# Ring slots by age, a router per token, and the first expert's rows gathered by quarters in a two-layer hybrid backbone

## The reference

```python
def _moe(h, router_w, w_gate, w_up, w_down):
    logits = (h @ router_w).astype(jnp.float32)
    top_v, top_i = lax.top_k(logits, TOP_K)
    top_w = jax.nn.softmax(top_v, axis=-1)
    gates = jnp.einsum('btk,btke->bte', top_w, jax.nn.one_hot(top_i, N_EXPERTS, dtype=jnp.float32)).astype(h.dtype)
    out = jnp.zeros_like(h)
    for e in range(N_EXPERTS):
        out = out + gates[..., e:e + 1] * _swiglu(h, w_gate[e], w_up[e], w_down[e])
    return out
...
        x = x + g1 * _rms_norm(y, norm_g[1])
        h2 = _modulate(_rms_norm(x, norm_g[2]), sh2, sc2)
        x = x + g2 * _rms_norm(ffn(h2), norm_g[3])
```

## Time and profile before

| what | us |
|---|---|
| median of 3 runs (1684.74 to 1691.21) | 1684.79 |
| profiled execution, its own time | 1685.35 |
| its span, first to last instruction | 1683.8 |
| TensorE busy | 1618.1 |
| VectorE busy | 1065.2 |
| ScalarE busy | 930.3 |
| mean granted clock of TensorE, share of full speed | 0.992 |

### The profile page before, as it was taken

One profiled execution on the slowest core, in us unless ns is written; L12 is line 12 of the kernel. 1 busy time (PEld: TensorE's weight loads), 2 busy tenths in 40 slices (PEclk: granted clock), 3 DMA queues, 4 the chain that ended last, 5 costly groups with the idle time before them and its releaser, 6 DMA issues.

```text
span 1683.8 us, 22722 instructions
## 1 busy us (share of the span) xinstructions
PE 1618.1 (96%) x8388; PEld 1296.7 (77%) x8388; DVE 1065.2 (63%) x1372; ACT 930.3 (55%) x1328; POOL 37.9 (2%) x60
## 2 busy tenths in 40 slices
PE   4999999899999999899997999999999999999997
PEld 2884469698888888688685888888888888888885
DVE  5442432532222333553655989999999999999998
ACT  4413332632222322552564777787778778787775
POOL 0000000040000000000001000000000000000000
PEclk9999999999999999999999999999999999999999
DMA  8623672696222222352134999999999999999982
GB/s 325 222 75 125 250 275 76 250 350 242 87 97 100 100 100 100 140 203 99 51 128 180 419 391 397 380 369 392 361 399 360 399 352 405 375 368 394 371 340 77
DMA packets 67850, 426.24 MB, mean 253 GB/s; under 512 B 8640, under 2 KB 12480, under 8 KB 19776
## 3 DMA queue, kind: packets, MB, share of 16 engines
q1 hardware_dynamic: 60000, 396.93, 61.2%
q0 software_dynamic: 7776, 28.32, 4.3%
HBM read 401.62 MB, written 23.59 MB: 253 GB/s over the span
## 4 chain that ended last, share of the span: by engine, by line
PE 91%; DVE 4%; ACT 2%; DMA 1%; issue 1%; SPq 0%; ACTq 0%; DVEq 0%
PE ps L1713 27%; PE ps L1715 26%; PE ps L1714 26%; PE ps L1731 2%; PE ps L1756 2%; PE ps L1888 1%; DMA raw<-in_w 1%; PE ps L2199 1%; PE ps L1949 1%; DVE small L1262 1%; PE ps L1932 1%; PE ps L1921 1%; DVE raw L1428 0%; DVE wl L1020 0%; PE ps L1953 0%
## 5 line engine op out<-in xcount | busy, mean ns | idle before, releaser
L1560 DVE TENSOR_TENSOR wl<-raw,wh 128x1024 fp32r<-128x1024 f32 x522 | 615.6, 1222 | 63.6 <-ACT wh L924 56.9
L924 ACT ACTIVATE wh<-raw 128x1024 fp32r<-128x1024 f32 x522 | 524.9, 1057 | 97.6 <-PE ps L1715 97.6
L1713 PE MATMUL ps<-wh,ah 128*128 128x512 f32 (+1 forms) x800 | 311.0, 389 | 2.3 <-issue 1.8
L1713 PE MATMUL ps<-ah,wh 128*128 128x512 f32 (+1 forms) x848 | 302.1, 356 | 9.5 <-DVE al L1137 6.0
L1715 PE MATMUL ps<-wh,al 128*128 128x512 f32 (+1 forms) x800 | 302.4, 378 | 0.0
L1714 PE MATMUL ps<-wl,ah 128*128 128x512 f32 (+1 forms) x800 | 301.6, 377 | 0.0
L1714 PE MATMUL ps<-al,wh 128*128 128x512 f32 (+1 forms) x848 | 293.8, 346 | 0.0
L1715 PE MATMUL ps<-ah,wl 128*128 128x512 f32 (+1 forms) x848 | 293.8, 346 | 0.0
L1020 DVE TENSOR_TENSOR wl<-raw,wh 128x1024 fp32r<-128x1024 f32 x120 | 141.6, 1221 | 116.9 <-ACT wh L500 116.9
L1713 PEld LDWEIGHTS ps<-ah,wh 128*128 128x128 f32 x848 | 161.4, 190 | 37.1 <-issue 6.9
L1714 PEld LDWEIGHTS ps<-al,wh 128*128 128x128 f32 x848 | 161.5, 190 | 20.4 <-issue 0.7
(11 more groups left out here) (260 smaller groups left out, 1489.1 us busy)
## 6 DMA issues: line engine op xcount, KB each, us to landing
raw<-in_w SPq DMA_DIRECT2D x372, 1024.0 KB, 6.2
sent<-raw POOLq DMA_DIRECT2D x16, 512.0 KB, 24.5
back<-raw POOLq DMA_DIRECT2D x16, 512.0 KB, 25.3
x<-sent POOLq DMA_DIRECT2D x7, 512.0 KB, 12.2
back<-x POOLq DMA_DIRECT2D x7, 512.0 KB, 8.6
x<-in_x SPq DMA_DIRECT2D x2, 1024.0 KB, 9.0
raw<-in_ukv SPq DMA_DIRECT2D x1, 1024.0 KB, 7.2
out<-raw SPq DMA_DIRECT2D x4, 256.0 KB, 3.3
```

The source lines that it names most:

```text
L924: act.activation(wh[:, J % SPLITS, piece_half(h)], slot(J % SLOTS)[:, piece_half(h)], ACT.Copy).then_inc(w_hi, 1)
L1560: ins = dve.tensor_tensor(wl[:, J % SPLITS, piece_half(h)], slot(J % SLOTS)[:, piece_half(h)], wh[:, J % SPLITS, piece_half(h)].bitcast(F3 ...
L1713: pe.matmul(out, lh, rh, start=start, stop=False)
```

## The change

**Slots.** `ring_slots` gives each ring entry the slot whose last entry is oldest, out of an allowed set. Fillers 14 to 30 and a few beside them may also use slots 7 and 8, once the projections have read them (`proj_ps`); fillers 31 to 39 and main 13 to 15 also slot 9, once the attention is over (`mla_pv`). The entries around layer one's feed-forward now wait for these:

| entry | slot before, waits for | slot after, waits for |
|---|---|---|
| main 13 | 1, main 12 split | 0, filler 28 used |
| main 14 | 1, main 13 split | 2, filler 32 used |
| filler 35 | 2, filler 33 used | 0, main 13 split |
| filler 36 | 0, filler 34 used | 1, filler 33 used |
| filler 37 | 1, main 14 split | 9, filler 34 used |
| filler 38 | 2, filler 35 used | 2, main 14 split |
| filler 39 | 0, filler 36 used | 0, filler 35 used |

SyncE issues in the order of the list, so an entry also waits for those ahead of it. ScalarE's split of main 14 moves ahead of the last two squares.

**Router.** The norm N_O2 with its sums on TensorE is gone. TensorE turns the unscaled `x` and multiplies it, per token, with a router that was multiplied by a beforehand. ScalarE squares the turned tokens with an accumulated sum per token, makes the root on two numbers per partition, and scales the turned tokens by it (`plain_tok`, no a, no b). The residual goes by pairs of chunks. `keep_busy` puts matmuls whose result nobody reads on TensorE at two places. The diagonal matrix, L2116 and `shiftB` are gone.

**Gather.** Expert 0's rows are gathered from `plain_tok` in four quarters in four banks; ScalarE applies a and b there (features are on partitions again) and rounds, VectorE takes the low part, and the first two pieces of `gate_up` wait for each quarter.

**Sent tokens.** They need a and b along the free axis. GpSimd writes a and b to memory (`flat_rows`) and reads them back to all partitions; VectorE multiplies and adds them after the selection, in between the quarters. Row numbers come after, the gates behind the first hidden product. The turn of the last expert's selection and the loads of the token count move to the end.

```diff
+        elif RING_AT["mod", ATT_MODS] <= p < RING_AT["main", M_GU + 3]:
+            allowed = OUT_SLOTS
+        last = {j: max([q for q in range(p) if slots[q] == j], default=-1) for j in allowed}
+        slots.append(min(allowed, key=last.get))
...
             out_unit(6)
+            split(M_GU + 1)
             for k in range(6, KD):
                 stream_square(N_E2L, k)
             root(N_E2L)
-            split(M_GU + 1)
...
+            for n, (a, b) in enumerate(ss_parts):
+                act.wait_ge(sem("tok_ps"), n + 1)
+                for t in range(2):
+                    act.activation(plain_part(t, a, b), by_pairs(turned(t, a, b)), ACT.Square, accum_out=tok_ss[:, t, n:n + 1]).then_inc(sem("tok_squared"), 1)
+            act.wait_ge(sem("tok_summed"), 1)
+            act.activation(tok_rinv, tok_sum, ACT.Ln, bias=eps[:, 0:1], scale=1.0 / D).then_inc(sem("tok_ln"), 1)
...
+                for k in range(KD):
+                    q, cols = k // 2, slice((k % 2) * P, (k % 2 + 1) * P)
+                    act.wait_ge(sem("first_ps"), q + 1)
+                    act.activation(xe_first[q][:, cols], ps[:, first_banks[q], cols], ACT.Identity,
+                                   bias=mod1[:, 24 + k, 0:1], scale=scl[:, 1, 2, k, 0:1]).then_inc(sem("xe_v"), 1)
...
+                counted(N_OY, p, dve.tensor_tensor(pair(tmp[p % 2]), y_o[:, two, :], rinv[:, None, 0:TL].broadcast_to([P, 2, TL]), ALU.mult))
+                dve.wait_ge(t_ready, T_AT[N_OY, p] + 1)
+                dve.tensor_tensor(x[:, two, 0:TL], x[:, two, 0:TL], pair(tmp[p % 2]), ALU.add).then_inc(res_done, 1)
...
+            def scaled_token(t):
+
+                dve.wait_ge(sem("rows_spread"), 16 * 2)
+                dve.wait_ge(sem("tok_f32"), 3 + t)
+                dve.tensor_tensor(tok_rows(t), plain_tok[t], scale_rows, ALU.mult).then_inc(sem("tok_scaled"), 1)
...
-                    first_gathered()
+                    scaled_token(0)
+                    scaled_token(1)
+                    first_gathered(0)
+                    shifted_token(0)
+                    first_gathered(1)
+                    shifted_token(1)
+                    first_gathered(2)
+                    row_numbers()
+                    first_gathered(3)
                     first_split(2)
                 split_next(0, AHEAD)
                 hidden(0, at.hid + 1)
                 if not no:
-                    dve.wait_ge(sem("back_sel_ps"), 1)
-                    dve.tensor_copy(back_sel_T, ps[:, 2, 0:TL]).then_inc(sem("back_sel_T"), 1)
+                    gates()
...
+            pool.wait_ge(sem("last_scales"), 1)
+            pool.wait_ge(w_used, M_OIN + OIN)
+            for n, columns in enumerate((scl[:, 1, 2, :, 0], mod1[:, 24:24 + KD, 0])):
+                pool.dma_start(flat_rows[n].rearrange("(k p) -> p k", p=P), columns, allow_slow_non_contiguous=True).then_inc(sem("rows_flat"), 16)
+            pool.wait_ge(sem("rows_flat"), 16 * 2)
+            for n, dst in enumerate((scale_rows, shift_rows)):
+                pool.dma_start(dst, flat_rows[n:n + 1, :].rearrange("o (a n) -> o a n", a=4).broadcast_to([P, 4, TL])).then_inc(sem("rows_spread"), 16)
...
             pe.wait_ge(evac_act, evacs(("t", 3), "act"))
+            keep_busy(6, 2)
             for k in range(KD):
-                sum_square(N_O2, k)
-                pe.wait_ge(sem("x_scaled"), k + 1)
-                mm = pe.matmul(ps[0:NE, 5, 0:TL], router[:, k, :], scaled_x[:, k, :], start=(k == 0), stop=(k == KD - 1))
...
+                for t in range(2):
+                    mm = pe.matmul(ps[:, 5, t * NE:(t + 1) * NE], x[:, k, t * P:(t + 1) * P], router[:, k, :], start=(k == 0 and t == 0), stop=(k == KD - 1 and t == 1))
+            mm.then_inc(sem("logits_ps"), 1)
+            keep_busy(6, 4)
```

More of the change, by code:

```diff
@@ L37 @@
 HEADS = 4
+N_PROJ = 2 * HEADS + HEADS // 2 + 4
 QR, KVR = 3, 2
@@ L99, with ring_slots @@
 FIRST_SLOTS = (7, 8, 3, 9, 0, 1, 2, 3, 9, 2)
-RING_SLOT = [FIRST_SLOTS[p] if p < len(FIRST_SLOTS) else (p - len(FIRST_SLOTS) + 1) % EARLY_SLOTS for p in range(len(RING))]
+ATT_SLOTS, OUT_SLOTS = (0, 1, 2, 7, 8), (0, 1, 2, 9)
+def ring_slots():
+    slots = list(FIRST_SLOTS)
+    for p, e in enumerate(RING):
+        if p < len(FIRST_SLOTS):
+            continue
+        allowed = tuple(range(EARLY_SLOTS))
+        if RING_AT["mod", NORM_MODS + 2] <= p < RING_AT["main", M_WOUT + 3]:
+            allowed = ATT_SLOTS
+        elif RING_AT["mod", ATT_MODS] <= p < RING_AT["main", M_GU + 3]:
+            allowed = OUT_SLOTS
+        last = {j: max([q for q in range(p) if slots[q] == j], default=-1) for j in allowed}
+        slots.append(min(allowed, key=last.get))
+    return slots
+RING_SLOT = ring_slots()
 VEC = {}
@@ L329, in build @@
         y_o = area(0, KD, TL)
-        scaled_x = x[:, :, TL:T]
+        plain_tok = [x[:, 4 * t:4 * t + 4, TL:T] for t in range(2)]
         xeh, xel = (a[:, 4:6, :].rearrange("p a b -> p (a b)").rearrange("p (k s) -> p k s", k=KD) for a in (ah, al))
@@ L354, in build, with by_pairs, plain_part, turned @@
         half_ss = small[:, 16:20]
+        tok_ss, tok_sum = small[:, 64:70].rearrange("p (t n) -> p t n", t=2), small[:, 72:74]
+        ss_parts = ((0, 4), (4, 6), (6, KD))
+        def by_pairs(v):
+            return v.rearrange("p (a n) -> p a n", n=TL)
+        def plain_part(t, a, b):
+            return plain_tok[t][:, a // 2:b // 2, :]
+        def turned(t, a, b):
+            bank, first = (2 * t, 0) if a < 4 else (2 * t + 1, 4) if a < 6 else (7 - 3 * t, 6)
+            return ps[:, bank, (a - first) * P:(b - first) * P]
         vecs_loaded = sem("vecs_loaded")
@@ L888, in _ @@
             root(N_OY)
-            for k in range(KD):
-                squares(N_O2, lambda k: x[:, k, 0:TL], lambda k: act.wait_ge(res_done, 4 * KD + k + 1), chunks=(k,))
-                act.activation(scaled_x[:, k, :], x[:, k, 0:TL], ACT.Copy, scale=scl[:, 1, 2, k, 0:1]).then_inc(sem("x_scaled"), 1)
-            root(N_O2)
+            for n, (a, b) in enumerate(ss_parts):
[4 more added lines that the diff above has]
+            act.activation(tok_rinv, tok_sum, ACT.Ln, bias=eps[:, 0:1], scale=1.0 / D).then_inc(sem("tok_ln"), 1)
+            act.wait_ge(sem("tok_ln"), 1)
+            act.activation(tok_rinv, tok_rinv, ACT.Exp, scale=-0.5).then_inc(sem("tok_root"), 1)
+            act.wait_ge(sem("tok_root"), 1)
+            for t, h in tok_parts:
+                for a, b in ss_parts[h:2 * h + 1]:
+                    ins = act.activation(plain_part(t, a, b), by_pairs(turned(t, a, b)), ACT.Copy, scale=tok_rinv[:, t:t + 1])
+                ins.then_inc(sem("tok_f32"), 1)
             act.wait_ge(sem("top_ready"), 1)
@@ L1737, in sum_squares, with keep_busy @@
                     sum_square(n, k)
+            def keep_busy(bank, times):
+                for _ in range(times):
+                    pe.matmul(ps[:, bank, :], ones, cst[:, 0:4, :].rearrange("p a b -> p (a b)"), start=True, stop=True)
             def out_pieces(first, W, n, ready=None):
@@ L2112, in _ @@
                       lambda u, b: pr_o[:, u % 2, 0, b * P:(b + 1) * P], early_norms, 1, 1)
-            pe.wait_ge(sem("diag_ready"), 1)
             pe.wait_ge(sem("diff_out"), len(ounits))
-            for k in range(KD):
-                mm = pe.matmul(ps[:, 6 + k // 4, (k % 4) * P:(k % 4 + 1) * P], ones, diag[:, k, :], start=True, stop=True)
-            mm.then_inc(sem("shift_ps"), 1)
             head_sums(DH // 2 - 1)
@@ L2176, in gate_up @@
                         kk = 4 * half + k
+                        if rows and kk % 2 == 0:
+                            pe.wait_ge(sem("first_xe_h"), kk // 2 + 1)
+                            pe.wait_ge(sem("first_xe_l"), kk // 2 + 1)
                         mm = mm3(ps[:, g % 2, :], xeh[:, kk, :], xel[:, kk, :], wh[:, b, k * 512:(k + 1) * 512],
@@ L2227, in experts @@
                 for half in range(2):
-                    if not no:
-                        pe.wait_ge(sem("first_xe_h"), half + 1)
-                        pe.wait_ge(sem("first_xe_l"), half + 1)
-                    gate_up(at.J + half, 0, half, 0)
+                    gate_up(at.J + half, 0, half, 0, rows=not no)
                 turn_hidden(0, at.hid + 1)
+                with pe.Fori(0, NE - 1) as e:
+                    body(e, ORDER, TURN)
                 if not no:
```

211 lines of the change are left out of this document (105 added, 106 removed).

## The result

The changed kernel takes 1670.84 us (median of 4 runs, 1669.60 to 1671.42), the kernel before 1685.24 beside it: a ratio of 0.9908, with a 95% interval of 0.9892 to 0.9923. 14.4 us are won; 15.2 were forecast. The profiled execution took 1671.42 us.

The account below looks back on a forecast made before the run. TensorE, busy 96% of the span, was taken as the bound, so only its idle time or removed work pays. 6.2 + 1.4 + 9.3 - 1.7 = 15.2 us won gives a median of 1669.6 us, range 1665.5 to 1676.5.

Parts of the forecast that it names:

- Term A: Ring slots near 300 us: fillers 35 to 37 no longer wait long for weights, context sum ends earlier; 6.2 us won.
- its six matmuls take 0.7, and the sum ends at 312.6: Half piece behind the modulated rows near 310 us: last step to the context sum, which before ended at 318.85.
- Term B: End of attention: third head sum starts when its squares are ready, no longer behind eight shift matmuls; 1.4 us won.
- Term C: Router chain, residual to first turn of the hidden rows: the turn comes at 914.15 instead of 923.41; 9.3 us won.
- Term D: Clock: one of two waits, at the experts' start or before the head sum, brings a half-clock stretch; 1.7 us lost.
- the bound of -3.4: Clock: the most to be lost to half-clock stretches, in us; the other bound was 0.
- The row transfers: GpSimd's writes and reads back of two 1024-number vectors: done before VectorE asks at 902.2, cost taken as 0.
- the upper bound: GpSimd's vector transfers: at most 2048 packets in 19 us and 256 wide ones in 2.4, leaving over 20 of 44 us.
- The covers: Experts' start: gates push the split of piece 4 to 919.1, 1 us of cover; last selection's turn costs 0.3 at the end.
- the ring pays little: Rival near 300 us: later loads or VectorE's modulation hold the half piece, gain falls to 2 us, 1674; chance 0.15.
- The keep-warm matmuls stand in the way: Rival in the router chain: at half clock the four matmuls take 6.9 us; 5 us lost, 1674.7; chance 0.17.
- The range's upper end: Whole kernel: 1676.5 us, if the two first rivals and a second clock stretch leave 8 to 9 us won.

Follow-up runs that it names:

- b_slots: Kernel before with the new ring slots only, the split of feed-forward piece 1 left behind the root on ScalarE; 1682.57 us, ratio 0.9972.
- b_ring: Kernel before with the new ring slots and the split of feed-forward piece 1 moved up on ScalarE, nothing else; 1682.20 us, ratio 0.9971.
- a_fillexp: Changed kernel with four more keep-warm matmuls behind the first expert's first two pieces, in the wait for the hidden product; 1669.05 us, ratio 0.9906.
- a_fillboth: Changed kernel with two keep-warm matmuls ahead of the first feed-forward half piece and four before the first turn of the hidden rows; 1668.37 us, ratio 0.9897.
- a_fillhead: Changed kernel with four more keep-warm matmuls in the wait before the third head sum; 1674.30 us, ratio 0.9918.
- a_warm2: Changed kernel with four keep-warm matmuls in place of eight ahead of the mask; 1671.59 us, ratio 0.9911.

## Why the prediction was right, step by step

The two profiled spans differ by 14.0 us. 1.4 of it is there at 242 us. Ahead of that point only the slots of fillers 14 to 30 differ, 0.9 of the 1.4 is there at 30 us already, and kernels that are the same there lie 3.9 us apart: I take it for chance between executions. The other 12.6 are 4.5 at the entry, 0.8 at the end of attention and 9.5 in the router stage, less 1.6 in the experts and 0.6 at the end of the program. That is 2.6 under the forecast of 15.2, with the mechanism as told. The median's 14.4 comes nearer, in part by luck: the kernel before, against which it is taken, had its router stage at 34.63 in this profile and 1.2 to 1.4 longer in b_slots and b_ring.

- **Term A, forecast 6.2, measured 4.5** (82.12 - 77.60), 4.8 in b_ring. The order was as told: fillers 35 to 37 without a wait over 1 us, the rows ready when forecast, and the moved split with the 2.53 us wait behind it untouched. The context sum was forecast at 312.6 by the clock of before, 311.2 on this trace, and ended at 312.36. The step that was mis-sized is "its six matmuls take 0.7, and the sum ends at 312.6", at full clock. In fact a half-clock stretch stood there. Where none did (a_fillexp, a_fillboth) the stage took 76.03, 6.1 us less than before: the term as forecast.
- **Term B, forecast 1.4, measured 0.8** (from the last rotation near 820 to the end of the output projection, 67.3 to 66.5). The head sum's half clock took the other part: with the wait filled (a_fillhead) that stage is 0.7 shorter still, 1.5 in all.
- **Term C, forecast 9.3, measured 9.5.** Inside it small errors cancelled. A router chunk took 0.62 to 0.69 and not 0.73; a quarter on ScalarE 1.15 and not 0.95, with VectorE's queue as forecast within 0.2. The wait at its end is 2.63, forecast 2.5. By single parts: the quarters carry 2.7 of the stage and the keep-warm matmuls 3.5. The router per token, without the sums of squares, and VectorE's new order were not run alone; what they carry is argued from the rows and not shown.
- **Term D, forecast -1.7 for one of two waits.** Both paid in the profiled execution: 0.7 behind the head sum (already within term B's 0.8), and 750.28 - 748.70 = 1.6 behind the turn, -2.3 together. The third stretch, near 308, was not forecast and cost 77.60 - 76.03 = 1.6 more, so the bound of -3.4 was passed too. The two granted clocks of the working, 0.88 and 0.70, are both of the stretch behind the wait of 2.32; the one behind 2.81 is told by its records only (0.86 us for two of 256 columns, 0.60 at full clock). What a stretch costs was right: the same experts took 748.64 without it (a_warm2) and 750.3 with it.
- **The row transfers, forecast 0:** right, with 68 us to spare where the bounds left over 20. The count under the upper bound was not: 96 packets for the two writes by the profile, 2048 assumed. Whether one packet holds many single elements no run here shows.
- **The covers.** The gates behind the hidden product pushed the split of piece 4 to 5.0 us behind the turn (912.21 less 907.20), as forecast (919.1 less 914.15), and no second wait came. Slot 9 landed 5.3 us before its split, where it had 12.2: less cover, none of it paid. At the end of the program 0.6 us was given back, 0.3 forecast.

Of the rivals, "the ring pays little" is refuted by b_ring. The row transfers were never near. "The keep-warm matmuls stand in the way" did not happen in the changed kernel, but it is real: a_fillhead's profile shows it at its price. Half clock under the eight came in three of the eight profiles that have them, at 4.4, 2.8 and 1.2 us (a_fillhead, a_fillexp, a_fillboth), though in neither profile of the changed kernel itself. So 0.17 was not too high, and that the tail of the stage before ran at full clock was thin evidence against it.

The range's upper end, 1676.5, does not follow from what is said for it: the two first rivals (4.2 and 5.1 us) with a second stretch (1.7) leave 4.2 of the 15.2 us, 1680.6. The result did not come near it.

## What to carry to other kernels

Size each term at both clocks. Where an engine waits for 1 to 3 us, the work behind it can come at full or half clock in two executions of one program, and the differences here (1.6 us a stretch, 4.4 where filler was in the way) are larger than most single edits.

That goes for filler too: four keep-warm matmuls ahead of the mask left a wait behind which the gather could run at half clock, eight took 6.5 us where the clock had fallen already. And when a queue is found to be what an engine waits for, move work within it before moving it to GpSimd, whose long passes can lock out VectorE's shortest operations.

Compare traces stage by stage between events that both have. Five to eight runs of one kernel lay 3 to 8 us apart between lowest and highest, and their medians could not have told 0.4 to 0.8 us of a moved split. But one profile's stage scatters as well, by 0.4 us at the entry and by 1.4 in the old router stage: read it against the same stage of every kernel that did not change it.

## What the runs showed that I had not expected

- The wait near 308, of 1.17 to 1.55 us, was followed by a half-clock stretch in eleven profiles and, at 1.18 us, by none in a_fillexp. That of 2.53 before the head sum was followed by one in seven profiles and by none in a_fillexp and a_fillboth. Waits of 1.96 and 1.97 us before the mask were followed by half and by full clock. The length of a wait alone does not decide. The prediction cited the Trainium skill ("TensorE: Matmul & The Clock Gate", What's actually happening) for this: the gate's own timing does not start with the kernel, so a wait may be caught in one run and not in the next. These profiles agree with it: a_fillexp's program is the changed kernel's up to its insertion near 902.
- Half-clock stretches also began with no long wait before them: in a_fillhead at 888.0, in the middle of the router's narrow matmuls, 2.8 us after a wait of only 0.58 had ended. It lasted 10.2 us.
- GpSimd's tensor_tensor over 1024 columns took 2.32 us, against VectorE's 1.18, and held VectorE's L1532 (0.17 us) for 2.27 and the two of L1536 (0.48) for 3.75.
- GpSimd's first two scatters, issued beside VectorE's weight splits, took 1.51 and 1.92 us, the next two 0.95 each. Before, the four took 0.95 to 1.02.
